# One step of a two-block network on one core: the experts' gate matrices by a split 256-column product

## The reference, cut to what matters

```
experts = e1 * N_KEYS + e2
gates = jax.nn.softmax(sv, axis=-1)
...
a = jnp.einsum('cd,ced->ce', h_c.astype(jnp.float32), u[e_c].astype(jnp.float32))
act = jax.nn.gelu(a, approximate=False) * g_c
return jnp.einsum('ce,ced->cd', act, v[e_c].astype(jnp.float32))
```

## Time and profile before

| what | value |
|---|---|
| median of 3 runs | 2585.79 us (2584.11 to 2585.95) |
| the profiled execution's own time | 2584.89 us |
| its span in the profile | 2582.8 us |
| PE busy | 2504.9 us, 97% |
| DVE busy | 1486.1 us, 58% |
| POOL busy | 1713.9 us, 66% |
| ACT busy | 674.3 us, 26% |
| mean granted clock of TensorE, share of full speed | 0.993 |

### The profile page before, as it was taken

The page is one execution under the profiler, slowest core; times in us unless marked ns, Lnnn a source line. Parts: engine busy times, 40 slices in busy tenths (PEclk is TensorE's granted clock), DMA queues, the critical chain, the costliest instruction groups (busy, mean ns, idle before and its releaser), DMA issues.

```text
span 2582.8 us, 35867 instructions
## 1 busy us (share of the span) xinstructions
PE 2504.9 (97%) x12919; PEld 2125.8 (82%) x12919; DVE 1486.1 (58%) x3290; ACT 674.3 (26%) x1215; POOL 1713.9 (66%) x1299
## 2 busy tenths in 40 slices
PE   6999999999999999999999999999999999999999
PEld 5876788888876676777788999999999978888887
DVE  7779521212413324433478897787778566666666
ACT  2137310101233424334110111111112233323332
POOL 3831476777552253474756678999997688888885
PEclk9989999999999999999999999999999999999999
DMA  9430122222221021221233348999997999999995
GB/s 381 188 114 17 50 98 98 84 98 95 88 77 49 33 71 48 82 98 66 83 121 113 127 171 300 330 336 356 366 348 271 343 368 346 352 345 352 351 350 207
DMA packets 134362, 501.85 MB, mean 194 GB/s; under 512 B 11232, under 2 KB 53600, under 8 KB 102752
## 3 DMA queue, kind: packets, MB, share of 16 engines
q1 hardware_dynamic: 70576, 311.71, 32.9%
q0 software_dynamic: 36864, 134.23, 13.7%
q10 hardware_dynamic: 26800, 54.32, 5.5%
HBM read 447.79 MB, written 52.43 MB: 194 GB/s over the span
## 4 chain that ended last, share of the span: by engine, by line
PE 74%; POOL 8%; DMA 7%; DVE 4%; issue 4%; ACT 1%; SPq 0%; ACTq 0%; DVEq 0%; POOLq 0%
PE banks L609 9%; PE banks L611 9%; PE banks L610 9%; PE banks L973 5%; PE banks L975 5%; PE banks L974 5%; PE banks L1058 3%; PE banks L1059 3%; PE banks L1060 3%; POOL W_lo L544 3%; DMA raw<-weights 3%; PE banks L778 3%; PE banks L796 2%; PE banks L1033 2%; POOL W_lo L467 2%
## 5 line engine op out<-in xcount | busy, mean ns | idle before, releaser
L492 POOL TENSOR_TENSOR W_lo<-raw,W_hi 128x512 fp32r<-128x512 f32 x376 | 495.9, 1329 | 0.0
L495 POOL TENSOR_TENSOR beat<-zero 128x1 f32<-128x1 f32 x94 | 19.2, 204 | 637.4 <-PE banks L611 208.5
L973 PE MATMUL banks<-A_hi,W_hi 128*128 128x384 f32 x1024 | 379.8, 371 | 1.1 <-issue 1.1
L975 PE MATMUL banks<-A_hi,W_lo 128*128 128x384 f32 x1024 | 345.9, 338 | 0.0
L974 PE MATMUL banks<-A_lo,W_hi 128*128 128x384 f32 x1024 | 344.3, 336 | 0.0
L467 POOL TENSOR_TENSOR W_lo<-raw,W_hi 128x2048 fp32r<-128x2048 f32 x65 | 299.6, 4609 | 5.2
L609 PE MATMUL banks<-A_hi,W_hi 128*128 128x512 f32 x680 | 268.4, 395 | 4.9 <-issue 4.9
L611 PE MATMUL banks<-A_hi,W_lo 128*128 128x512 f32 x680 | 265.6, 391 | 0.0
L610 PE MATMUL banks<-A_lo,W_hi 128*128 128x512 f32 x680 | 265.4, 390 | 0.0
L487 POOL CAST W_hi<-raw 128x512 fp32r<-128x512 f32 x376 | 248.3, 675 | 0.0
L2057 DVE TENSOR_TENSOR A_lo<-arena,A_hi 128x768 fp32r<-128x768 f32 x64 | 136.9, 2140 | 164.8 <-ACT A_hi L1498 164.7
(11 more groups left out here) (315 smaller groups left out, 5982.9 us busy)
## 6 DMA issues: line engine op xcount, KB each, us to landing
raw<-weights SPq DMA_DIRECT2D x221, 1024.0 KB, 4.9
gelu_dram<-B_plain ACTq DMA_DIRECT2D x64, 384.0 KB
gates_dram<-arena ACTq DMA_DIRECT2D x48, 512.0 KB, 10.3
arena<-gelu_dram SPq DMA_DIRECT2D x32, 768.0 KB, 8.4
arena<-gates_dram SPq DMA_DIRECT2D x30, 768.0 KB, 11.1
arena<-weights SPq DMA_DIRECT2D x15, 1024.0 KB, 10.2
B_lo_plain<-weights SPq DMA_DIRECT2D x5, 1024.0 KB, 21.0
B_plain<-weights SPq DMA_DIRECT2D x4, 1024.0 KB, 17.8
```

Of the source, the lines that this page charges most:

```text
L492: return pool.tensor_tensor(W_lo[:, j, cols], raw[:, j, cols], W_hi[:, j, cols].bitcast(F32), ALU.subtract)
L973: mm(to, lh, rh, start=k == 0, stop=False)
L975: last = mm(to, ll, rh, start=False, stop=k == KD - 1)
```

## The change

A token's gate matrix is now made by one float32r matmul with 256 columns. The first operand is the one-hot matrix of e1 in float32r (`hot_first`). The second operand (`hot_second`) has two halves of 128 columns: the one-hot of e2 times the high half of the gate, and the same times its low half. So PSUM receives two 128x128 matrices a token, which have to be added. Two tokens now fill a bank.

- DVE, for each group of four tokens: one comparison of 128x512 for e2, written to PSUM bank 0 or 1 (`plain_hot`); one comparison of 128x512 for e1, written to SBUF (`first_hot`). Both compare the row 0..127 with picks, and the row has moved from PSUM to SBUF (`iota_sb`), as banks 0 and 1 are now written. DVE also takes the gate matrices out of PSUM (`gates_out`): of each four tokens two by an addition of the high part onto what ACT has copied, and two by a `tensor_reduce` over the two parts; in the last block all by `tensor_reduce`.
- ACT, for each token: two scalings of the plain one-hot of e2 from PSUM by the high and the low half of the gate (`scaled`), and for two of four tokens the copy of the low part (`low_out`). ACT also makes the high halves of 40 slabs of u (`slab_high`), each ahead of the gelu of the slab before it. It issues no transfers in this stage any more.
- POOL makes only the low half of those 40 slabs; for the others it goes on casting.
- SP issues the stores of the gelus and of the gates (`store_gelus`, `store_gates`), the gates of a block behind the gelus of the slab it is named with.

```diff
-            def one_hot(t, j):
-                dve.wait_ge(hot_used, t + (j + 1))
-                e1, e2, gate = (picks_t[:, i, bass.ds(t + j, 1)] for i in range(3))
-                dve.tensor_scalar(hot[j][0], iota_psum, e1, None, ALU.is_equal)
-                dve.tensor_scalar(hot[j][1], iota_psum, e2, gate, ALU.is_equal, ALU.mult)\
-                    .then_inc(hot_ready, 1)
+            iota_sb = ident_r[:, :].bitcast(F32)
+            def compared(group, i):
+                return (iota_sb.unsqueeze(1).to_broadcast([P, GROUP, KEYS]),
+                        picks_t[:, i, GROUP * group:GROUP * group + GROUP].unsqueeze(2).to_broadcast([P, GROUP, KEYS]))
+            def plain_hot(group):
+                if group >= 2:
+                    dve.wait_ge(hot_ready, GROUP * (group - 1))
+                to = bank[group % 2][:, :].rearrange("p (t e) -> p t e", t=GROUP)
+                dve.tensor_tensor(to, *compared(group, 1), ALU.is_equal).then_inc(plain_ready, 1)
+            def first_hot(group):
+                dve.wait_ge(hot_used, GROUP * group + GROUP)
+                slot = GROUP * group % HOTS
+                dve.tensor_tensor(hot_first[:, slot:slot + GROUP, :], *compared(group, 0), ALU.is_equal)\
+                    .then_inc(first_ready, GROUP)
+            def gates_out(t):
+                q, j = t // GT, t % GT
+                out_ = stage_of(q)[:, :, j:j + 2]
+                both = bank[4 + t // 2 % 2][:, :].rearrange("p (t h e) -> p e t h", t=2, h=2)
+                if q == GB - 1 or j % GROUP:
...
+                    dve.wait_ge(hot_used, t + 2 + HOTS)
+                    dve.tensor_reduce(out_, both, AX, ALU.add).then_inc(g_copied, 2)
+                else:
+                    dve.wait_ge(low_copied, t // GROUP + 1)
+                    dve.tensor_tensor(out_, out_, both[:, :, :, 0], ALU.add).then_inc(g_copied, 2)
...
+            for group in range(TD // GROUP):
+                plain_hot(group)
+                due = min(SLOTS, GROUP * (group + 1) * DOTS // DOT_TOKENS)
+                if group >= 2:
+                    gates_out(GROUP * (group - 2))
+                if due > k:
+                    dot(k)
+                    k += 1
+                if group >= 2:
+                    gates_out(GROUP * (group - 2) + 2)
+                first_hot(group)
+                if due > k:
+                    dot(k)
+                    k += 1
```

On PE, ACT, POOL and SP:

```diff
-                            if j % 4 == 0:
-                                pe.wait_ge(g_copied, t + (GT * q + j + 4))
+                            if j % 2 == 0:
+                                pe.wait_ge(g_copied, t + (GT * q + j + 6))
+                            if j % GROUP == 0:
+                                pe.wait_ge(first_ready, t + (GT * q + j + GROUP))
                             pe.wait_ge(hot_ready, t + (GT * q + j + 1))
-                            mm(bank[4 + j // 4 % 2][:, P * (j % 4):P * (j % 4) + P], hot[j % HOTS][0],
-                               hot[j % HOTS][1], start=True, stop=True).then_inc(hot_used, 1)
+                            to = bank[4 + j // 2 % 2][:, 2 * P * (j % 2):2 * P * (j % 2) + 2 * P]
+                            mm(to.rearrange("p (h e) -> p h e", h=2), hot_first[:, j % HOTS, :],
+                               hot_second[j % HOTS], start=True, stop=True).then_inc(hot_used, 1)
...
+            def slab_high(w):
+                act.wait_ge(slab_loaded[w % 2], (w - w % 2) * 8 + 16)
+                act.wait_ge(slab_used, w - 1)
+                act.activation(W_hi[:, w % 2, :], raw[:, w % 2, :], ACT.Copy).then_inc(u_high, 1)
             def gelus(s, odd=0, tokens=None):
...
+                if isinstance(s, int) and U_AT <= s < U_AT + HIGH_BY_ACT:
+                    slab_high(N_MID + s + 1)
...
+            def scaled(group, parts):
+                act.wait_ge(plain_ready, group + 1)
+                for i in parts:
+                    t = GROUP * group + i
+                    second, plain = hot_second[t % HOTS], bank[group % 2][:, P * i:P * i + P]
+                    act.wait_ge(hot_used, t + 1)
+                    act.activation(second[:, 0, :], plain, ACT.Copy, scale=picks_t[:, 2, t:t + 1])
+                    act.activation(second[:, 1, :], plain, ACT.Copy, scale=gate_low[:, t:t + 1]).then_inc(hot_ready, 1)
+            def low_out(t):
...
+                act.wait_ge(hot_used, t + 2 + HOTS)
+                both = bank[4 + t // 2 % 2][:, :].rearrange("p (t h e) -> p h e t", t=2, h=2)
+                act.activation(stage_of(q)[:, :, j:j + 2], both[:, 1, :, :], ACT.Copy).then_inc(low_copied, 1)
...
             def split_whole(s):
                 j = s % 2
-                pool.wait_ge(slab_loaded[j], (s - j) * 8 + 16)
-                pool.wait_ge(slab_used, s - 1)
-                pool.tensor_copy(W_hi[:, j, :], raw[:, j, :]).then_inc(slab_half, 1)
-                pool.wait_ge(slab_half, s + (IN_PARTS * (PARTS - 1) + 1))
+                if HOT_AT < s <= HOT_AT + HIGH_BY_ACT:
+                    pool.wait_ge(u_high, s - HOT_AT)
+                else:
+                    pool.wait_ge(slab_loaded[j], (s - j) * 8 + 16)
+                    pool.wait_ge(slab_used, s - 1)
+                    pool.tensor_copy(W_hi[:, j, :], raw[:, j, :]).then_inc(slab_half, 1)
+                    own_halves[0] += 1
+                    pool.wait_ge(slab_half, own_halves[0])
                 low_of(s)
...
+            def store_gelus(s):
+                sp.wait_ge(gelu_ready, 2 * s + 2)
+                sp.dma_start(gelu_dram[s, :, :, :], gelu_out[:, 2 * (s % 2):2 * (s % 2) + 2, 0:TD])\
+                    .then_inc(gelu_stored[s % 2], 16)
...
+                    store_gelus(first + s)
+                    if s < with_tokens:
+                        per_slab = STORES // (2 if q == GB - 1 else 4)
+                        for part in range(per_slab * s, min(STORES, per_slab * s + per_slab)) if q else ():
+                            store_gates(q - 1, part)
+                    else:
+                        for part in range(STORES // 2 * (s - with_tokens), STORES // 2 * (s - with_tokens + 1)):
+                            store_gates(q, part)
```

More of the change, by code:

```diff
@@ L56 @@
 U_GOT, V_GOT = 6, 8
+GROUP = 4
+HIGH_BY_ACT = KD * 5
 STORES = 8
@@ L149, in build @@
                 pass
+        with nc.sbuf_tensor("arena_before_hot", [P, ARENA - HOTS * KEYS], F32):
+            with nc.sbuf_tensor("hot_first", [P, HOTS, KEYS], F32R) as hot_first:
+                pass
         arena = sb("arena", [P, ARENA])
@@ L406, in _ @@
                     load_ada(s)
-            tail = (base - N_ADA) % 2
-            with sp.Fori(LOADED_FIRST, base - N_ADA - tail - 1, 2) as s:
+            ahead = N_MID + U_AT + 3
+            assert (ahead - LOADED_FIRST) % 2 == 0
+            with sp.Fori(LOADED_FIRST, ahead - 1, 2) as s:
                 for j in range(2):
@@ L434, in gates_of, with store_gates @@
                     .then_inc(pair_loaded[d], 16)
[L436 to L442, removed]
+            def store_gelus(s):
+                sp.wait_ge(gelu_ready, 2 * s + 2)
+                sp.dma_start(gelu_dram[s, :, :, :], gelu_out[:, 2 * (s % 2):2 * (s % 2) + 2, 0:TD])\
+                    .then_inc(gelu_stored[s % 2], 16)
+            def store_gates(q, part):
+                if part == 0:
+                    sp.wait_ge(g_copied, 8 + GT * (q + 1))
+                e = KEYS // STORES
+                sp.dma_start(g_dram[q][:, e * part:e * part + e, :].rearrange("p e t -> p (e t)"),
+                             g_stage[:, q % 2, GT * e * part:GT * e * part + GT * e])\
+                    .then_inc(g_stored[q % 2], 16)
+            first = U_AT
+            for q, (with_tokens, between) in enumerate(U_BLOCKS):
+                for s in range(with_tokens + between):
+                    w = N_MID + first + s + 3
+                    if w < base - N_ADA:
+                        sp.wait_ge(slab_split, w - 1)
+                        load_slab(w)
+                    elif w == base - N_ADA:
+                        value_slab(0, 0)
+                    elif w == base - N_ADA + 1:
+                        sp.wait_ge(g_stored[0], 8 * STORES * GB)
+                        sp.wait_ge(g_stored[1], 8 * STORES * (GB - 2))
+                        for d in range(2):
+                            gelus_of(0, d)
+                            gates_of(0, d, GB - 1)
+                        value_slab(0, 1)
+                    store_gelus(first + s)
[6 more added lines that the diff above has]
+                            store_gates(q, part)
+                first += with_tokens + between
             for s in range(2, PAIRS, 2):
@@ L1445, in _ @@
             act.drain().then_inc(g_copied, 8)
[L1446 to L1453 removed]
+            act.activation(hot_first[:, 4:7, :], picks_t[:, 2, :].rearrange("p (i t) -> p i t", i=3), ACT.Copy)\
+                .then_inc(gate_high, 1)
@@ L1456, in _ @@
             for q, (with_tokens, between) in enumerate(U_BLOCKS):
```

(16 more changed lines are left out.)

50 lines of the change are left out of this document (23 added, 27 removed).

## The result

The changed kernel takes **2701.43 us** (median of 4 runs, 2697.92 to 2705.36) against 2585.87 us for the kernel before: ratio 1.0447, 95% interval 1.0429 to 1.0465. It is slower, as predicted, but lies 55 us above the forecast of 2646 and 11 us above the upper end of the range. The profiled execution took 2697.92 us, its span is 2696.1 us, 113.3 us more than before.

A forecast was written before the change was run, and what follows sets the result against it. PE was taken to bound the kernel before (busy 97%), DVE held by POOL the changed u stage. Start 3, five blocks 42, last block 10 and end 6 gave +61 us on 2584.9, so 2646 us; range 2590 to 2690.

The forecast's parts named there:

- the hold: u stage: DVE comparisons with two SBUF inputs wait for POOL's low half, 3.5 us a slab in the mean.
- the prediction's 11.45: First five blocks of u: 11.45 us a slab against 10.41 before, +42 us over 40 slabs.
- The phase: Five blocks: low half holds the next group's first comparison 4.2 us in three of five cases, otherwise the second 2.6.
- PE: u stage: a 256-column token matmul costs 0.12 us, so PE needs 9.28 us a slab, 10.24 in the last block.
- The rival without holds: u stage: broadcast operands do not collide with POOL, PE's pace rules; -43 us, 2543 us; chance 0.12.
- POOL's slab 8.7 us, below 11.45: u stage: POOL's low half and 3.2 gathers take 8.7 us a slab, so POOL adds nothing.
- the edits at nothing: u stage: ACT's 8.1 us a slab, SP's issues of 0.5 us each and POOL's 8.7 us add no time.
- forecast 7.93: Five blocks: DVE's own comparisons, additions, reductions and dots take 7.93 us a slab without being held.
- if DVE's waits fall together with waits it would have anyway: u stage: one of two conditions under which the forecast fails; no size given.
- The rival of the worst phase: u stage: every low half meets a waiting comparison, 12.53 and 16.1 us a slab; +114 us, 2700; chance 0.1.
- the last block: Last block of u, no dots: 13.7 to 16.1 us a slab, taken as 14.6 against 12.09; +10 us.
- Start and end: u stage: chain ahead of the first token +3 us (2 to 4); later gate stores at the end +6 (0 to 9).

The follow-up runs named there:

- e2: Not a run in this text: the token's pick whose one-hot is scaled by the gate's halves; the run e2_short_low (2565.59 us) is not cited.
- e10: The changed kernel with two of a slab's gathers issued ahead of POOL's low half, comparisons still reading two SBUF inputs; 2661.82 us.
- e1: As a run: the changed kernel with both comparisons reading the row 0..127 from PSUM again, every other group's plain one-hots going to SBUF; 2632.66 us.
- e6: e1 with POOL issuing two of a slab's gathers ahead of its wait for the high half; 2551.19 us.

## Why the prediction was right in sign and short in size

Four kernels make a square:

| | gathers behind the low half | two gathers ahead of it |
|---|---|---|
| comparisons from SBUF, held | 2701 us | 2662 us |
| row in PSUM, not held | 2633 us | 2551 us |

**Right: the hold.** Comparisons of 0.68 us last up to 5 and end just behind POOL's low half, though two of their operands are broadcast. The Trainium skill's page "SBUF — State Buffer", section "Who interferes with whom", says the same of such operations in general; the comparisons agree. By itself, in the kernel with gathers ahead, the hold costs 2662 - 2551 = 111 us, measured from PE's pace. The 11.61 us a slab are near the prediction's 11.45 in part by luck: a hold of 3.5 us was forecast and no wait, 2.62 us of hold and 0.95 of waits were there. The phase was half right: in 20 of 40 slabs a comparison for e2 is held, by 4.1 us in the mean (forecast 4.2 us in three of five), and the comparison for e1 in 19, by 1.15 us (forecast 2.6).

**Right: PE.** A token of 256 columns costs 0.12 us: the token matmuls of one half stand 0.64 us apart with three of 384 columns between them (0.52).

```profile
2091.28 0.28 PE L1083 MATMUL banks<-A_hi,hot_first 128*128 128x256 f32 x1
...
2091.92 0.28 PE L1083 MATMUL banks<-A_hi,hot_first 128*128 128x256 f32 x1
```

The rival without holds was put at 2543 us; without hold and loop the kernel takes 2551.

**Failed: "POOL's slab 8.7 us, below 11.45", among the edits at nothing.** POOL's work fits, and that was all I asked. I had not asked who stands behind POOL's new wait for ACT's high half (the gathers), nor what stands on DVE behind the dots that wait for those gathers (the operations that empty PE's banks, which ACT did before). The changed kernel's own rows show the failed term: in the five blocks DVE waits 2.74 us a slab, 1.97 of them for gathered rows, where the prediction had nothing. The hold adds only 1.72 us a slab there and not 3.5: the comparison for e2 is held in 10 of 40 slabs. The rest of the 12.56 us, 8.1, is the operations themselves (forecast 7.93). The closing sentence of the prediction, that it fails "if DVE's waits fall together with waits it would have anyway", had half of it: beside each other both shrink, but as the waits for rows stood at nothing in the sum, the slab came out longer and not shorter. The rival of the worst phase had 2700 us, which is near the result, but not for its reason: without the loop the hold costs 11.61 us a slab, and not its 12.53. Here the loop costs 12.56 - 11.61 = 0.95 us a slab, 37 us in the five blocks; 2701 against 2662 for the whole kernel. Where nothing is held it costs 2633 - 2551 = 81 us. The two don't add (150 us together, 111 + 81 = 192 from each alone). The rows agree: from e10 to the changed kernel the hold falls from 2.62 to 1.72 us a slab, and from e1 to the changed kernel DVE's waits for rows fall from 114 to 78 us. The reading, that rows arrive while DVE is held and low halves pass while it waits for rows, is argued and not tested by itself.

**Mis-sized: the last block.** 17.7 us a slab against 14.6, and against 16.1 as the worst phase. It is the same in e10 (17.7) and falls to 10.21 in e1, so it is all hold and what follows from it. The comparisons of the block last 5.5 us a slab beyond 0.68 us (forecast 5.0), and DVE waits some 12 us in the four slabs for PE's tokens, which the forecast had at nothing. The chain is in the timeline: the comparison for e2 is held for 5.00 us at 2097.78 (shown above); ACT's scaling waits 4.95 us for it, and PE 5.01 us for ACT:

```profile
2102.82 0.37 ACT L1515 ACTIVATE A_hi<-banks,arena 128x128 fp32r<-128x128 f32 x1 [4.95 <-DVE banks L2089]
...
2103.51 0.57 PE L1083 MATMUL banks<-A_lo,hot_first 128*128 128x256 f32 x1 [5.01 <-ACT A_hi L1516]
...
2103.88 0.52 PE L1020 MATMUL banks<-A_hi,W_hi 128*128 128x384 f32 x1
...
2104.20 0.52 PE L1021 MATMUL banks<-A_lo,W_hi 128*128 128x384 f32 x1
...
2108.39 0.34 PE L1021 MATMUL banks<-A_lo,W_hi 128*128 128x384 f32 x1
2108.56 0.33 PE L1022 MATMUL banks<-A_hi,W_lo 128*128 128x384 f32 x1
```

**Missing: the clock.** After a gap of 5 us PE's matmuls of 384 columns start 0.32 us apart (2103.88 to 2104.20) and not 0.17, the 1.2 GHz level, until about 2107.7, then (2108.39 to 2108.56) at full speed again. Such 4 us at half speed lose about 2 us in each slab of the last block, which is most of the 3.1 us that the forecast was short there (an estimate from these rows). In the five blocks the granted clock is 0.90 to 0.93, in e1 0.94 to 0.95, in e6 0.99 to 1.00. What that alone costs there isn't parted from the gaps that bring it.

**Start and end.** The start was mis-sized too, though the first gelu is only 2.1 us later (forecast 3, bounds 2 and 4). The profiled execution of the changed kernel ends the stretch before it, whose work is the same, 4.3 us earlier. These are the last gelu of that stretch before and after, and the first token's matmul after:

```profile
1549.56 0.49 ACT L1418 ACTIVATE B_plain<-banks 128x384 f32<-128x384 f32 x1 [3.67 <-PE banks L975]
```

```profile
1545.22 0.49 ACT L1476 ACTIVATE B_plain<-banks 128x384 f32<-128x384 f32 x1 [3.67 <-PE banks L1022]
...
1556.34 0.58 PE L1083 MATMUL banks<-A_hi,hot_first 128*128 128x256 f32 x1 [2.41 <-DVE hot_first L2095]
```

From there to the first gelu of the stage it is 11.56 us before and 17.95 after, so the start costs 6.4 us. PE stands for 2.41 us until the first comparisons are done, and its matmuls of 384 columns start 0.32 us apart until 1561.6, the lower clock level again. All kernels here with high halves on ACT take 16.6 to 18.0 us for this; their stretch before it ends anywhere from 1545.2 to 1552.0, so the 4.3 us are taken as scatter between executions.

The end cost 3.2 us (forecast 6, bounds 0 and 9); the eleven other kernels with this end have 547.4 to 551.0 us behind the last gelu, so this is known to a few us only. The last store was issued behind the stage's last matmul, as said, but POOL's first gather of v follows it by 6.7 us (2158.32 - 2151.59) instead of the 14.8 us of the earlier trace rows:

```profile
2147.90 3.69 SPq L455 DMA_DIRECT2D gates_dram<-arena  x4
```

```profile
2158.32 0.97 POOL L565 DMA_INDIRECT arena<-v_rows,arena  x1 [4.91 <-DMA gates_dram<-arena]
```

**The sum.** Against the forecast's span of 2643.8 us: five blocks +42.9 (37.3 the loop, 5.6 the hold), last block +12.5, two slabs +0.6, start +3.4, the stretch before it -4.3, end -2.8: 52.3 us in all.

**The scalings on ACT** last 0.37 to 0.40 us in the median and not 0.28 as taken from the earlier trace rows, but start 0.25 us apart. ACT has room for them (61% busy), and in e6 they don't show.

## What to carry to other kernels

Before an operand is moved from PSUM to SBUF, ask which POOL operation runs beside its readers: here one move of a 128-column row made DVE stand for up to 5 us, and putting it back was worth 69 us, or 111 us once the gathers were ahead. Where a change adds a wait to an engine, go through everything queued behind it, small issues such as gathers above all, and on to whoever waits for those; an engine that frees PSUM banks should not have waits for transfers ahead of that work in its queue. Busy sums per slab only say that a loop can be closed, not how long one turn of it takes; a gap on PE then costs more than its length, since the matmuls after the gaps of 5 us here ran at half speed for some 4 us.

## What was not expected of the hardware

The hold works in the other direction as well. POOL's gathers lasted 1112 and 1101 ns in the mean beside held comparisons, and 943 and 944 ns in e1, with the row in PSUM (groups of POOL, first after, then e1):

```profile
L565 POOL DMA_INDIRECT B_lo_plain<-u_rows,arena x70 | 77.9, 1112 | 18.1 <-issue 11.9 <-DVE B_lo_plain L2115 3.4 <-DVE B_plain L2115 1.5
L565 POOL DMA_INDIRECT B_plain<-u_rows,arena x35 | 38.5, 1101 | 8.8 <-issue 6.3 <-DVE B_lo_plain L2115 1.8
```

```profile
L568 POOL DMA_INDIRECT B_lo_plain<-u_rows,arena x73 | 68.8, 943 | 18.8 <-issue 14.8 <-DVE B_lo_plain L2117 1.1 <-DVE B_plain L2117 0.9
L568 POOL DMA_INDIRECT B_plain<-u_rows,arena x37 | 34.9, 944 | 9.3 <-issue 7.9 <-DVE B_lo_plain L2117 0.6
```

The Trainium skill's page "SBUF — State Buffer" infers, in the section named above, that DVE operations of this kind leave descriptor generation alone. The instruction that issues a gather does last longer beside them, here and in the earlier trace rows, and the rows decide; which part of it waits they don't show. At 0.16 us a gather and some 3 gathers a slab it costs half a microsecond a slab of a POOL that has room, so it isn't in the sum.
